# The causal mask as the first instead of the last product of each score bank in two key-block attentions

## The chip, the cores and the metric

The kernel runs on one core of a Trainium2 chip. The metric is the device time of one execution in microseconds, smaller is better. The kernel before took 2220.15 us as the median of three runs (2218.11 to 2220.37).

## What is computed

A float32 transformer of a first block (forgetting attention and stick-breaking attention side by side, then a mixture of 16 experts) and two more layers, the second of which mixes tokens with a native sparse attention (NSA). 512 tokens, width 1024. The change touches two attentions. The forgetting attention has 8 heads of 64:

```
logits = einsum(q, k) * scale + F[t] - F[s]      # F: running sum of log forget gates
logits = where(kpos <= qpos, logits, -inf)
out    = softmax(logits) @ v
```

NSA has 16 heads in 4 groups and adds three attentions by gates: over compressed keys, over selected key blocks and over a window. With 512 tokens there are 8 blocks of 64 and 16 may be selected, and the window is 512 wide, so the last two are plain causal attentions over their own keys and values, with a slope on the distance:

```
sc = einsum(q_blk, ks) * scale - slopes * dist
sc = where(dist >= 0, sc, NEG)
p  = softmax(sc)
```

## The kernel before

All engines run one long program each; the order of the work on each is the order in which it is written out, and semaphores join them. TensorE (PE) makes all products. To keep float32 accuracy a product is split in high and low parts (fp32r, one cycle a column), for instance the helper at L1729 with its three products; a product of two plain float32 tiles runs in two passes of two cycles a column.

Both attentions work by key blocks of 128 keys. For head h and key block j, a score bank (a PSUM bank, 128 keys by the 512 - 128 j queries from the block on) collects three products: the high keys with the high queries (L1990 in the forgetting attention, L2487 in NSA), the low terms (L1991, L2488), and a mask (L1995, L2495), which is an identity `IDB` as weights times `LKB`, 128x128 in bfloat16, with large negative numbers where a key lies after a query. It touches only the first 128 columns, the block on the diagonal. Its semaphore (`fs_done`, `s_done`) lets ScalarE (ACT) take the exponential (L1082, L1484) into `PROB`. The weighted product (L2004, L2514) of plain float32 `PROB` with the values follows two blocks later in the forgetting attention and three blocks later in NSA. Three score banks are used in turn; the scores of block n wait for the exponential of block n - 3.

The row of maxima that goes into the queries of a head is made two heads ahead: maxima products (L1947, L2438; for the compressed keys L2431) into another bank, CMB masks (L1956, L2449: `IDB` times `CMB`, bfloat16) on top, a reduction on VectorE (DVE, L2880, L3474), four small products that turn the maxima into a row (L1968, L2461), and a copy by ACT (L1062, L1439). L1980 and L2470 spread weights over partitions. ACT also moves finished outputs (L1070, L1071, L1449, L1450).

One turn n of the loop before: score products of block n, maxima products for head h + 2 (forgetting: turns 0 to 2 of 4; NSA: turns 0 to 6 of 9, turn 6 without CMB masks), the LKB mask of block n, the CMB masks, sometimes a spread or the row of maxima, then the weighted product of the older block. In NSA blocks 0 to 3 and 4 to 7 of a head are the two causal branches, block 8 the compressed one, which has no LKB mask. The last two heads have no maxima left to make.

The choice of banks relies on the first product of a bank with `start=True`: it opens the whole bank, and a later product writes what has not been written since and adds elsewhere. The maxima banks already use that.

Of the kernel before, what the change touches and what calls it, by code (L numbers as in the profile page):

```python
# [29 lines left out]
P = 128  # L30
D = 1024
T = 512
# [132 lines left out]
def program(nc, a, out):  # L165


    def sb(name, shape, dt=F32):
        return nc.alloc_sbuf_tensor(name, shape, dt)

    def sem(name):
        return nc.alloc_semaphore(name)
# [20 lines left out]
    IDB = sb("IDB", [P, P], BF16)  # L193
# [20 lines left out]
    PB = [nc.alloc_psum_tensor(f"PB{i}", [P, T], F32) for i in range(8)]  # L214
# [67 lines left out]
    def slot(n, kk=KK, width=W):  # L282
        if kk == KK and width == W:
# [22 lines left out]
    fs_done, fp_done, fpv_blk, fo_free = (sem(f"fox_{x}") for x in  # L306
                                                   ("scores", "probs", "block_used", "out_moved"))
# [36 lines left out]
    s_done, p_done, pv_blk, o_free = (sem(f"nsa_{x}") for x in ("scores", "probs", "block_used", "out_moved"))  # L344
# [89 lines left out]
    LKB = sb("LKB", [P, P], BF16)  # L434
# [13 lines left out]
    def over(name, start, shape, dt=F32):  # L448

        return nc.alloc_sbuf_tensor_at(name, shape, dt, offset=start)  # L450
# [33 lines left out]
    NQA, NQB = over("NQA", ht_at, [P, 4, T], F32R), over("NQB", htl_at, [P, 4, T], F32R)  # L484
# [15 lines left out]
    FKA, FKB = over("FKA", big_at, [P, NH1, T], F32R), over("FKB", big_at + 4096 * F, [P, NH1, T], F32R)  # L500
    FQA, FQB = over("FQA", big_at + 8192 * F, [P, 4, T], F32R), over("FQB", big_at + 10240 * F, [P, 4, T], F32R)
# [19 lines left out]
    NSA_BLOCKS = [(h, b, j) for h in range(NSA_H) for b in range(3) for j in range(1 if b == 2 else NT)]  # L521
# [12 lines left out]
    with block as blk:  # L534
# [1145 lines left out]
        def _(pe):  # L1680
# [136 lines left out]
            for d in range(ND):  # L1817
                if d > 5:
                    pe.wait_ge(n_ht[0], d - 5)
                for i in range(NT):  # L1820
                    if d == 0:
                        pe.wait_ge(n_xn, i + 1)
                    ins = pe.transpose(PB[XT_BANK[d]][:, i * P:(i + 1) * P], XN[:, i, d * P:(d + 1) * P], IDENT[:, :])
# [97 lines left out]
            for k in range(ND):  # L1921
                for n, (w, x) in enumerate(((FWH, HTH), (FWH, HTL), (FWL, HTH))):
                    ins = pe.matmul(PB[4][0:NH1, :], w[:, k, :], x[:, k, :], start=(k == 0 and n == 0),
                                    stop=(k == ND - 1 and n == 2))
# [14 lines left out]
            def fox_maxima(h, turn):  # L1939

                n = 3 * h + turn
                bank = PB[1 + n % 2]
                if n >= 2:
                    pe.wait_ge(fm_max, n - 1)
                for i in MAX_PARTS[turn]:
                    at_ = 384 if (turn, i) == (1, 0) else 0
                    pe.matmul(bank[:, at_:at_ + (i + 1) * P], FQA[:, h % 4, i * P:(i + 1) * P],  # L1947
                              FKA[:, h, 0:(i + 1) * P], start=(i == MAX_PARTS[turn][0]), stop=False, skip_group_check=True)

            def fox_max_masks(h, turn):  # L1950

                n = 3 * h + turn
                bank = PB[1 + n % 2]
                for i in MAX_PARTS[turn]:
                    at_ = 384 if (turn, i) == (1, 0) else 0
                    ins = pe.matmul(bank[:, at_ + i * P:at_ + (i + 1) * P], IDB[:, :], CMB[:, :], start=False, stop=True,  # L1956
                                    skip_group_check=True)
                ins.then_inc(fm_done, 1)
# [23 lines left out]
            def fox_scores(n):  # L1982

                h, j = FOX_BLOCKS[n]
                dst, q0 = PB[(0, 3, 4)[n % 3]][:, 0:T - j * P], j * P
                if n >= 3:
                    pe.wait_ge(fp_done, n - 2)
                if j == 0:
                    pe.wait_ge(fm_row, h + 1)
                pe.matmul(dst, FKA[:, h, q0:q0 + P], FQA[:, h % 4, q0:T], start=True, stop=False)  # L1990
                pe.matmul(dst, FKB[:, h, q0:q0 + P], FQB[:, h % 4, q0:T], start=False, stop=False)  # L1991

            def fox_score_mask(n):

                pe.matmul(PB[(0, 3, 4)[n % 3]][:, 0:P], IDB[:, :], LKB[:, :], start=False, stop=True).then_inc(fs_done, 1)  # L1995

            def fox_weighted(n):

# [21 lines left out]
            for n in range(len(FOX_BLOCKS) + 2):  # L2020
                h, t = n // NT, n % NT
                if n < len(FOX_BLOCKS):
                    fox_scores(n)
                    if h + 2 < NH1 and t < 3:
                        if t == 0:
                            pe.wait_ge(fq_ready, h + 3)
                        fox_maxima(h + 2, t)
                    fox_score_mask(n)
                    if h + 2 < NH1 and t < 3:
                        fox_max_masks(h + 2, t)  # L2030
                    if 1 <= h < NH1 - 1 and t == 1:
                        fox_max_T(h + 1)
                    if (h, t) in SPREAD_AT:
                        fox_spread(SPREAD_AT[h, t])
                if n >= 2:
                    fox_weighted(n - 2)
# [80 lines left out]
            for half in range(2):  # L2117
                g, q0 = GR["gates"] + 4 * half, 12 * half
# [57 lines left out]
            ins = pe.matmul(PB[5][:, 0:NT * EXPERTS], ONES[:, 0:P], chosen, start=True, stop=True)  # L2176
# [114 lines left out]
            for k in range(ND):  # L2291
                for n, (w, x) in enumerate(((KRH, HTH), (KRH, HTL), (KRL, HTH))):
                    ins = pe.matmul(PB[4][0:32, :], w[:, k, :], x[:, k, :], start=(k == 0 and n == 0),
                                    stop=(k == ND - 1 and n == 2))
# [49 lines left out]
            for m in range(2):  # L2344
                pe.wait_ge(m_qn if m == 0 else m_kn, 1 if m == 0 else 1 + NT)
                for h in range(MLA_H):
# [5 lines left out]
                    for i in range(NT):  # L2352
                        src = QN[:, i, h * QK_D:(h + 1) * QK_D] if m == 0 else KN[:, i, h, :]
                        ins = pe.transpose(PB[h][0:QK_D, i * P:(i + 1) * P], src, IDENT[:, :])
# [30 lines left out]
            for k in range(ND):  # L2385
                for n, (w, x) in enumerate(((SWGH, HTH), (SWGH, HTL), (SWGL, HTH))):
                    ins = pe.matmul(PB[0][0:48, :], w[:, k, :], x[:, k, :], start=(k == 0 and n == 0),
                                    stop=(k == ND - 1 and n == 2))
# [31 lines left out]
            for m in range(2):  # L2420
                ins = pe.transpose(PB[2][0:DH, m * CMP_LEN:(m + 1) * CMP_LEN], PER[:, m, :], IDENT[0:CMP_LEN, 0:CMP_LEN])
# [50 lines left out]
            def scores(n):  # L2472

                h, b, j = NSA_BLOCKS[n]
                if n >= 3:
                    pe.wait_ge(p_done, n - 2)
                if b == 0 and j == 0:
                    pe.wait_ge(mrow_ready, h + 1)
                grp = h // NSA_R
                if b == 2:  # L2480
                    dst, q0 = PB[n % 3][0:96, :], 0
                    keys = (t[:, grp, :, :].rearrange("p r n -> p (r n)") for t in (KCA, KCB))
                else:
                    dst, q0 = PB[n % 3][:, 0:T - j * P], j * P
                    keys = NKA[:, b * NSA_G + grp, q0:q0 + P], NKB[:, b * NSA_G + grp, q0:q0 + P]
                high, low = keys
                pe.matmul(dst, high, NQA[:, h % 4, q0:T], start=True, stop=False)  # L2487
                ins = pe.matmul(dst, low, NQB[:, h % 4, q0:T], start=False, stop=(b == 2))  # L2488
                if b == 2:
                    ins.then_inc(s_done, 1)  # L2490

            def score_mask(n):

                if NSA_BLOCKS[n][1] < 2:
                    pe.matmul(PB[n % 3][:, 0:P], IDB[:, :], LKB[:, :], start=False, stop=True).then_inc(s_done, 1)  # L2495

            def weighted(n):

# [18 lines left out]
            def token_products(m, l):  # L2517

                z = ZS[m][:, :, 2 * l:2 * l + CMP_STRIDE * (NCMP - 1) + 1:CMP_STRIDE]
                dst = PB[m][0:DH, 0:NSA_G * NCMP].rearrange("p (a b) -> p a b", a=NSA_G)  # L2520
                return pe.matmul(dst, CWS[:, m, l, :], z, start=(l == 0), stop=(l == CMP_LEN // 2 - 1))  # L2521
# [14 lines left out]
            for l in range(CMP_LEN // 2):  # L2536
                ins = token_products(0, l)
# [5 lines left out]
            for l in range(CMP_LEN // 2):  # L2543
                ins = token_products(1, l)
# [5 lines left out]
            for m in range(2):  # L2550
                for l in range(CMP_LEN // 2):
                    ins = position_products(m, l)
# [3 lines left out]
            for turn_no in range(len(SECOND_MAXIMA_AT), 6):  # L2556
# [3 lines left out]
                      start=True, stop=True).then_inc(c_mm, 1)  # L2560
            for q in range(NSA_G):
                ins = pe.matmul(PB[6][0:NCMP, q * DH:(q + 1) * DH], HD[:, 1, q, :], CW2[:, 1, :], start=True, stop=True)
# [7 lines left out]
            for n in range(len(NSA_BLOCKS) + 3):  # L2570
                h, t = n // PER_HEAD, n % PER_HEAD
                if n < len(NSA_BLOCKS):
                    scores(n)
                    if h + 2 < NSA_H and t < len(MAX_TURNS):
                        if t == 0:
                            pe.wait_ge(q_ready, h + 3)
                        maxima(h + 2, *MAX_TURNS[t])
                    score_mask(n)
                    if h + 2 < NSA_H and t < len(MAX_TURNS):
                        max_masks(h + 2, *MAX_TURNS[t])  # L2580
                    if h % 2 and h >= 3 and t in (1, 3, 5):
                        spread((h - 3) // 2, t // 2)
                    if h + 2 < NSA_H and t == PER_HEAD - 1:
                        max_T(h + 2)
                if n >= 3:
                    weighted(n - 3)
# [1006 lines left out]
```

## Time and profile before

| | |
|---|---|
| median of three runs | 2220.15 us |
| span of the profiled execution | 2216.6 us (3.55 us below the median; the runs' times take in what lies around the span) |
| PE busy | 96% of the span |
| ACT, DVE busy | 43%, 55% |
| forgetting attention, key blocks | about 121 to 162 us |
| NSA, key blocks | about 1623 to 1801 us |

Times in the rows count from the span's start. Each matmul appears twice: its weight load on PEld and its product on PE. The product's recorded duration runs to the end of its results, so that following products overlap; the distance from one start to the next is the better measure of what a product takes.

### The profile page before, as it was taken

The numbers are of one execution on the slowest core, as the hardware profiler recorded it, in microseconds if no ns is written. First come the engines' busy times: TensorE is split into PE (matmuls) and PEld (weight loads), VectorE is DVE, ScalarE is ACT, GpSimd is POOL, SyncE is SP. The second block draws the span as 40 slices with busy tenths as digits, with TensorE's granted clock in tenths as the row PEclk, the third lists the DMA queues.
The fourth block names the chain that finished last, engine by engine and source line by source line (L and its number), as shares of the span: only waits on it lengthen the run. The fifth ranks groups of instructions, "written<-read, shape, count | busy, mean of one in ns | idle before, by whom it ended". The sixth has DMA issues, their size and how long they took to land.

```text
span 2216.6 us, 25820 instructions
## 1 busy us (share of the span) xinstructions
PE 2132.4 (96%) x10108; PEld 1670.4 (75%) x10108; DVE 1211.2 (55%) x1702; ACT 953.0 (43%) x1484; POOL 188.3 (8%) x239
## 2 busy tenths in 40 slices
PE   8999999999999968999999999999999999999998
PEld 4768678867676647887878888878877767888887
DVE  6747654477777745367544454453446555445444
ACT  4455532346655524236431134343357765112343
POOL 2240001101000010000000000020223200000000
PEclk9999999999999988999999999999989999999999
DMA  9405035939999973220223322232100012332221
GB/s 350 162 25 177 9 127 176 364 133 354 383 379 373 383 270 99 91 79 27 77 90 104 101 95 95 95 106 95 60 1 3 3 50 86 98 102 94 102 99 58
DMA packets 153080, 309.05 MB, mean 139 GB/s; under 512 B 15062, under 2 KB 16619, under 8 KB 152957
## 3 DMA queue, kind: packets, MB, share of 16 engines
q1 hardware_dynamic: 122788, 229.98, 30.4%
q0 software_dynamic: 11648, 41.60, 4.9%
q10 hardware_dynamic: 18524, 35.81, 4.6%
q8 instruction: 81, 1.33, 0.2%
q14 instruction: 39, 0.32, 0.0%
HBM read 275.97 MB, written 30.99 MB: 138 GB/s over the span
## 4 chain that ended last, share of the span: by engine, by line
PE 84%; DVE 7%; DMA 4%; ACT 4%; issue 1%; POOL 0%; SPq 0%; ACTq 0%; DVEq 0%; POOLq 0%
PE PB L1729 60%; PE PB L2246 4%; PE PB L2514 3%; DMA BIG<-in_expert_w_down 3%; PE PB L2488 1%; PE PB L2438 1%; PE PB L2487 1%; PE PB L1881 1%; PE PB L1902 1%; PE PB L2004 1%; DVE WL L2657 1%; PE PB L2186 1%; PE PB L2521 1%; PE PB L2075 1%; DMA X<-in_x 1%
## 5 line engine op out<-in xcount | busy, mean ns | idle before, releaser
L2657 DVE TENSOR_TENSOR WL<-RING,WH 128x1024 fp32r<-128x1024 f32 x228 | 280.7, 1231 | 595.2 <-ACT WH L970 384.3
L970 ACT CAST WH<-RING 128x1024 fp32r<-128x1024 f32 x228 | 239.4, 1050 | 769.2 <-PE PB L1729 764.4
L1729 PE MATMUL PB<-HTH,WH 128*128 128x512 f32 x1056 | 412.2, 390 | 4.8 <-DVE HTL L2684 3.7
L1729 PE MATMUL PB<-HTL,WH 128*128 128x512 f32 x1056 | 411.0, 389 | 0.0
L1729 PE MATMUL PB<-HTH,WL 128*128 128x512 f32 x1056 | 410.9, 389 | 0.0
L1729 PEld LDWEIGHTS PB<-HTH,WH 128*128 128x128 f32 x1056 | 198.4, 188 | 48.1 <-issue 5.5
L1729 PEld LDWEIGHTS PB<-HTH,WL 128*128 128x128 f32 x1056 | 198.3, 188 | 41.5
L1729 PEld LDWEIGHTS PB<-HTL,WH 128*128 128x128 f32 x1056 | 198.4, 188 | 40.3
L1729 PE MATMUL PB<-WH,NHH 128*128 128x512 f32 x496 | 193.2, 390 | 1.8 <-DVE NHL L2662 1.8
L1729 PE MATMUL PB<-WL,NHH 128*128 128x512 f32 x496 | 193.0, 389 | 0.0
L1729 PE MATMUL PB<-WH,NHL 128*128 128x512 f32 x496 | 193.0, 389 | 0.0
L3051 DVE TENSOR_TENSOR EWL<-RING,EWH 128x1024 fp32r<-128x1024 f32 x128 | 151.8, 1218 | 50.3 <-ACT EWH L1186 49.9
L1186 ACT CAST EWH<-RING 128x1024 fp32r<-128x1024 f32 x128 | 130.7, 1049 | 86.6 <-PE PB L1729 71.6
L1729 PE MATMUL PB<-EWH,HTL 128*128 128x512 f32 x512 | 166.9, 407 | 0.0
L1729 PEld LDWEIGHTS PB<-EWH,HTL 128*128 128x128 f32 x512 | 93.9, 188 | 24.1 <-issue 6.7
L1729 PEld LDWEIGHTS PB<-WH,NHH 128*128 128x128 f32 x496 | 93.1, 188 | 21.7 <-DVE NHL L2662 2.6
L2246 PE MATMUL PB<-BIG,NAT 128*128 128x512 f32 x240 | 106.7, 594 | 2.4 <-DMA BIG<-in_expert_w_down 2.3
L1729 PEld LDWEIGHTS PB<-WH,NHL 128*128 128x128 f32 x496 | 93.1, 188 | 19.4
L1729 PEld LDWEIGHTS PB<-WL,NHH 128*128 128x128 f32 x496 | 93.1, 188 | 19.4
L1729 PE MATMUL PB<-WH,HTL 128*128 128x512 f32 (+1 forms) x296 | 99.6, 367 | 1.0 <-DVE BIG L3376 1.0
L1729 PE MATMUL PB<-EWL,HTL 128*128 128x512 f32 x256 | 100.3, 392 | 0.0
L2514 PE MATMUL PB<-PROB,NVA 128*128 128x512 f32 (+3 forms) x256 | 95.7, 456 | 1.7 <-ACT RST L1450 1.0
(594 smaller groups left out, 3453.5 us busy)
## 6 DMA issues: line engine op xcount, KB each, us to landing
RING<-in_mlp_w SPq DMA_DIRECT2D x64, 1024.0 KB, 5.1
RING<-in_expert_w_gate SPq DMA_DIRECT2D x32, 1024.0 KB, 7.8
RING<-in_expert_w_up SPq DMA_DIRECT2D x32, 1024.0 KB, 12.0
BIG<-in_expert_w_down ACTq DMA_DIRECT2D x30, 1024.0 KB
RING<-in_w_in SPq DMA_DIRECT2D x20, 1024.0 KB, 5.2
BIG<-in_ada_w SPq DMA_DIRECT2D x9, 2048.0 KB, 13.8
dispatch_rows<-BIG POOLq DMA_DIRECT2D x24, 512.0 KB, 18.6
RING<-in_a_w_in SPq DMA_DIRECT2D x10, 1024.0 KB, 5.1
```

Of the source, the lines that this page charges most:

```text
L970: ins = nc.scalar.copy(split_weights(stage, q)[0], halves_of(n, q))
L1186: nc.scalar.copy(EWH[:, q % MOE_SLOTS], halves_of(CH["moe"] + GU_AT[e] + j // 2, j)).then_inc(high_ready, 1)
L1729: yield pe.matmul(dst, lhs, rhs, start=(start and n == 0), stop=(stop_ and n == 2))
L1881: ins = pe.matmul(PB[u % 4][:, 0:nk + nk % 2], lhs, rhs, start=(n == 0), stop=(n == len(pairs) - 1))
L1902: ins = pe.matmul(PB[6 + u % 2][:, 0:DH], PT[0:n, u % 2, j, :], v(it, h, b, j, n), start=(j == 0), stop=(j == len(m) - 1))
L2004: ins = pe.matmul(PB[5 + h % 2][:, j * P:T], v, PROB[:, n % 4, 0:T - j * P], start=(j == 0), stop=(j == NT - 1))
L2075: ins = pe.matmul(PB[3 + 4 * (p % 2)][half, i * P:(i + 1) * P], SV[:, j, h * DH:(h + 1) * DH], SPT[:, u % 4, j, :], start=(j == 0), stop=( ...
L2186: ins = pe.matmul(PB[banks[d // 4]][:, (d % 4) * P:(d % 4 + 1) * P], NAT[:, i, d * P:(d + 1) * P], hits[:, i, :], start=(i == 0), stop=(i ...
L2246: ins = pe.matmul(PB[5 + m][:, :], ACTT[e % 2][:, k, :], w[:, k, :], start=(k == 0), stop=(k == KK - 1))
L2514: ins = pe.matmul(dst, lhs, rhs, start=(j == 0), stop=last)
L2657: return V.tensor_tensor(wl, halves_of(n, q), wh.bitcast(F32), ALU.subtract)
L3051: V.tensor_tensor(EWL[:, q % MOE_SLOTS], halves_of(CH["moe"] + GU_AT[e] + j // 2, j), EWH[:, q % MOE_SLOTS].bitcast(F32), ALU.subtract).th ...
```

## The change

The LKB mask product moves from behind the maxima products to the first place of its turn. It opens the bank (`start=True`), both score products add to it, and the low product closes it and gives the semaphore. The block with compressed keys is as before. `skip_group_check=True` concerns the build alone.

```diff
@@ forgetting attention, fox_scores
-                pe.matmul(dst, FKA[:, h, q0:q0 + P], FQA[:, h % 4, q0:T], start=True, stop=False)
-                pe.matmul(dst, FKB[:, h, q0:q0 + P], FQB[:, h % 4, q0:T], start=False, stop=False)
-
-            def fox_score_mask(n):
-
-                pe.matmul(PB[(0, 3, 4)[n % 3]][:, 0:P], IDB[:, :], LKB[:, :], start=False, stop=True).then_inc(fs_done, 1)
+                pe.matmul(dst[:, 0:P], IDB[:, :], LKB[:, :], start=True, stop=False, skip_group_check=True)
+                pe.matmul(dst, FKA[:, h, q0:q0 + P], FQA[:, h % 4, q0:T], start=False, stop=False, skip_group_check=True)
+                pe.matmul(dst, FKB[:, h, q0:q0 + P], FQB[:, h % 4, q0:T], start=False, stop=True,
+                          skip_group_check=True).then_inc(fs_done, 1)
@@ its loop, between the maxima products and the CMB masks
-                    fox_score_mask(n)
@@ NSA, scores
-                pe.matmul(dst, high, NQA[:, h % 4, q0:T], start=True, stop=False)
-                ins = pe.matmul(dst, low, NQB[:, h % 4, q0:T], start=False, stop=(b == 2))
-                if b == 2:
-                    ins.then_inc(s_done, 1)
-
-            def score_mask(n):
-
-                if NSA_BLOCKS[n][1] < 2:
-                    pe.matmul(PB[n % 3][:, 0:P], IDB[:, :], LKB[:, :], start=False, stop=True).then_inc(s_done, 1)
+                if b < 2:
+                    pe.matmul(dst[:, 0:P], IDB[:, :], LKB[:, :], start=True, stop=False, skip_group_check=True)
+                pe.matmul(dst, high, NQA[:, h % 4, q0:T], start=(b == 2), stop=False, skip_group_check=True)
+                pe.matmul(dst, low, NQB[:, h % 4, q0:T], start=False, stop=True, skip_group_check=True).then_inc(s_done, 1)
@@ its loop, between the maxima products and the CMB masks
-                    score_mask(n)
```

## Rows read from the trace of the kernel before

**Rows 1.** The page: span, busy time, and the chain that ended last by engine.

```profile
span 2216.6 us, 25820 instructions
PE 2132.4 (96%) x10108; PEld 1670.4 (75%) x10108; DVE 1211.2 (55%) x1702; ACT 953.0 (43%) x1484; POOL 188.3 (8%) x239
PE 84%; DVE 7%; DMA 4%; ACT 4%; issue 1%; POOL 0%; SPq 0%; ACTq 0%; DVEq 0%; POOLq 0%
```

**Rows 2.** Busy time by stretch (us), with counts, granted PE clock, DMA share, GB/s.

```profile
121.00:162.00 41.00, 39.66 (x240) 28.18 (x241) 16.76 (x29) 25.64 (x54) 13.91 (x18) 1.00 0.01 2
1623.00:1801.00 178.00, 176.19 (x1042) 131.18 (x1042) 96.23 (x206) 133.67 (x267) 41.28 (x48) 0.98 0.02 3
```

**Rows 3.** Waits, 1623 to 1801: who waited for whom: us, times, longest.

```profile
ACT PROB L1484 <- PE PB L2495: 38.0, 62, 1.5
PEld PB L2487 <- ACT PROB L1484: 2.5, 10, 0.3
PE PB L2514 <- ACT RST L1450: 1.0, 2, 0.7
PE PB L2461 <- ACT NQA L1439: 0.8, 1, 0.8
```

**Rows 4.** Timeline, weight loads, 1685.9 to 1687.3: start, us, what.

```profile
1686.17 0.10 PEld L2495 LDWEIGHTS PB<-LKB,IDB 128*128 128x128 bf16 x1
1686.19 0.15 PEld L2449 LDWEIGHTS PB<-CMB,IDB 128*128 128x128 bf16 x2
1686.30 0.30 PEld L2514 LDWEIGHTS PB<-PROB,NVA 128*128 128x128 f32 x2
1686.73 0.19 PEld L2487 LDWEIGHTS PB<-NQA,NKA 128*128 128x128 f32 x1
1687.06 0.19 PEld L2488 LDWEIGHTS PB<-NQB,NKB 128*128 128x128 f32 x1
```

**Rows 5.** Timeline, 1689.25 to 1689.66: a mask with no CMB masks behind it.

```profile
1689.34 0.19 PEld L2488 LDWEIGHTS PB<-NQB,NKB 128*128 128x128 f32 x1
...
1689.52 0.10 PEld L2495 LDWEIGHTS PB<-LKB,IDB 128*128 128x128 bf16 x1
...
1689.52 0.31 PEld L2514 LDWEIGHTS PB<-PROB,NVA 128*128 128x128 f32 x2
```

**Rows 6.** Chain that ended last, 1786 to 1801 (NSA heads 14 and 15).

```profile
1795.49 0.46 ACT OUP L1449
...
1796.57 1.04 ACT CWH L1457
```

**Rows 7.** Turn 3 of even heads: timeline about 1695.5, chain at first and last.

```profile
1695.16 0.57 ACT L1450 COPY RST<-PB 1x512 f32<-1x512 f32 x1
...
1695.48 0.10 PEld L2449 LDWEIGHTS PB<-CMB,IDB 128*128 128x128 bf16 x1
...
1695.85 0.30 PEld L2514 LDWEIGHTS PB<-PROB,NVA 128*128 128x128 f32 x2 [0.27 <-issue]
...
1650.50 0.12 issue
...
1763.61 0.12 issue
```

**Rows 8.** Chain, 120 to 162: L1990 at turn 0 of heads 1 to 5.

```profile
125.51 0.23 PE PB L1990
...
130.44 0.47 PE PB L1990
...
135.60 0.35 PE PB L1990
...
140.66 0.47 PE PB L1990
...
145.82 0.35 PE PB L1990
```

**Rows 9.** Busy time by stretch as in rows 2; granted clock third from the end.

```profile
1620.00:1640.00 20.00, 19.02 (x105) 14.44 (x105) 8.70 (x20) 11.49 (x22) 3.43 (x4) 0.79 0.00 1
1640.00:1660.00 20.00, 19.88 (x122) 14.87 (x121) 8.62 (x21) 14.70 (x31) 6.11 (x8) 1.00 0.02 3
```

## The prediction

> **What bounds the kernel now.** I read first the page, to see which engine sets the time: TensorE (PE) is busy in 96% of a span of 2216.6 us and makes up 84% of the chain that ended last [rows 1]. Then the stretches in which the changed lines run: 121 to 162 us (forgetting attention, 8 heads of 4 key blocks) and 1623 to 1801 us (the 16 NSA heads, 9 blocks each). PE is busy for 39.7 of 41 and 176.2 of 178 us, ScalarE (ACT) for 25.6 and 133.7 [rows 2]. In both stages one turn of the loop is: score products, maxima products two heads ahead, masks, weighted product of an older block. The waits of the NSA stage name ACT waiting for the score mask (38.0 us, 62 times), but PE's weight loads waiting for an exponential only for 2.5 us and PE for a moved output or row 1.8 us [rows 3]. So the exponential has slack, and what counts is how many nanoseconds of PE each turn takes. An earlier score bank is worth little; an order that costs PE more is paid in full.
>
> **How PE's turn is read.** Busy matmul rows overlap and say nothing of spacing; the weight loads (PEld) do. The load of the next matmul begins when the matmul before begins to stream. In [rows 4] L2487 is loaded at 1686.73, while the second pass of L2514 streams 384 columns at two cycles each (0.32 us); L2488 is loaded at 1687.06: no gap, the f32 load is hidden. Where a 128-column matmul is in front, it is not: after the last CMB load (the second of the pair from 1686.19, so about 1686.24) the first L2514 load follows at 1686.30, one mask's streaming later (0.06), but its second load only 0.11 after that (two loads of 0.19 take 0.30 in all). A load of f32 weights thus takes 0.11 us of PE where no longer matmul covers it; a bf16 load takes no more than the 0.06 us that a mask streams.
>
> **A mask in company and a mask alone.** In company (LKB mask, then CMB masks) another bf16 mask costs 0.06 us: it shifts the rest by its own columns, and the one uncovered f32 load is paid by the last mask whoever that is. Alone between two f32 matmuls, as at the turns without CMB masks [rows 5]: L2488 is loaded at 1689.34, so streams from 1689.45 (0.11 later, its own load being uncovered) to 1689.50 (128 columns, 0.05). The mask's load starts only then, at 1689.52; the next f32 matmul's second load, the start of its streaming, is at 1689.64 (0.31 less 0.19 after 1689.52). So from stream to stream a lone mask costs 0.13 us.
>
> **The change part by part.** The products are the same: 160 masks, 160 pairs of score products, no DMA, nothing else on another engine. Opening the bank with 128 columns and adding the products to it I cost at nothing, since the second product already adds to a bank at its column count. The waits (probability, row of maxima) stay ahead of the turn's first matmul, now the mask: nothing new queues behind them. What moves is the mask.
> 1. Turns with CMB masks: 6 of 9 in NSA heads 0 to 13 (84), 3 of 4 in forgetting heads 0 to 5 (18). The mask leaves its company (-0.06) and stands alone between L2514 (L2004) and L2487 (L1990), whose load was hidden (+0.13): +0.075 each by the unrounded spacing. 84 give 6.3 us, 18 give 1.35.
> 2. Turns whose mask was alone already, behind a 128-column product: NSA turns 6 and 7 of heads 0 to 13 (28), forgetting turn 3 of heads 0 to 5 (6). Before: 0.05 + 0.13 from the last product's start to the next. After: 0.11, for the f32 load behind 128 columns is still uncovered. Minus 0.07, plus 0.13 in front: +0.06 each, 1.7 and 0.35 us. Turns of NSA heads 14 and 15 with 256 or more columns change place with place: nothing; there the chain runs through ACT (0.46 OUP, 1.04 CWH) anyway [rows 6], so their 128-column turns cost nothing either.
> 3. Stalls that this fills. At turn 3 of every second NSA head (2 to 12, six times) L2514 waits for ACT to move the output of the branch before: the CMB load is at 1695.48, L2514's at 1695.85 instead of 1695.54, 0.12 after the RST copy ends; the chain shows the same 0.12 of issue at 1650.50 and 1763.61, first and last of the six [rows 7]. Two turns lie between that branch's last product and the wait; PE comes 0.15 us later and waits 0.15 less: -0.9 us. In the forgetting stage L1990 stands on the chain for 0.47 us (130.44, 140.66) or 0.35 (135.60, 145.82) where it needs 0.23 (125.51) [rows 8]: it waits for its row of maxima. A mask that comes first takes over that gap; ACT's row comes no later and PE arrives later: -0.7 us.
> 4. The first 8 us of the NSA stage run at half clock (granted 0.79 over 1620 to 1640, 1.00 after) [rows 9]: the exposed loads double there for half a head, +0.2 us.
>
> Sum: 6.3 + 1.7 - 0.9 + 1.35 + 0.35 - 0.7 + 0.2 = **+8.3 us**. After both stages the chain goes on with PE's split matmuls, so it arrives whole: the profiled span would be 2224.9, and the median, 3.5 us above this span, 2220.15 + 8.3 = 2228.4 us.
>
> **The bounds.** No row shows a bf16 load behind a plain-f32 matmul of two passes (L2514), nor a lone mask ahead of L2487. From below, the mask costs 0.06 there as in company: items 1 and 2 vanish or turn slightly negative, about 2219 to 2220 us. From above, the whole recorded f32 load (0.19) lies open behind the mask: 0.20, that is 0.07 more in 136 turns, +9.5, about 2238 us. I take 0.13: rows 5 are the same pair, mask before f32, and the bf16 load that begins only at the end of a stream is seen after f32 products whatever their width.
> The Trainium skill, "TensorE: Matmul & The Clock Gate" (Step-by-step: what each phase is for), says that PE pulls the next weight load ahead of matmuls in flight into a background buffer, so that it runs under the current one. Taken alone this would hide the mask's load and leave only its streaming, the lower bound; rows 4 show it for f32 behind long matmuls, rows 5 show it failing for a bf16 load behind f32.
>
> **Rivals.**
> - **No change (chance 0.12).** The switch is free in the new place: L2514's passes are long (128 to 512 columns, two cycles each) and may cover the bf16 load and, with it, part of the next. A lone mask then costs 0.06, the sum is 0 to +2: 2219 to 2222. For it: rows 4, hidden f32 load. Against it: rows 5, and a 128-column mask cannot cover a load of 0.11.
> - **Faster (0.05).** The score banks close before the maxima instead of after them: on average 427 columns (0.18 us) and a mask earlier, in 102 turns. If PE were waiting for probabilities in most turns, up to 0.23 x 102 = 23 us would come back; less 9.9 of added load, 13.6 us faster, 2206.6. It decides once PE waits for exponentials in about half of the turns (0.23 x 51 is more than 9.9). The rows give 2.5 us in all for that wait [rows 3], so only PE idle that the profile does not show could bring it.
> - **Slower through the clock (0.07).** The stage begins with some 8 us at half clock [rows 9]; a PE with more gaps could stay there as long again, which costs half of it, +4.2: 2232.6.
> - **Forecast (0.76)**, its own range 2224 to 2232.
>
> **How the numbers follow.** A measurement of this kernel tells about 0.2% (4.4 us) from nothing. Slower by more than that, over 2224.6, takes nearly all of the forecast and the clock case: 0.82. Within: the no-change case and the forecast's low edge, 0.13. Faster: 0.05. The range leaves out the far ends of the bounds and the faster case: 2222 to 2234.
>
> **What would show it.** In the NSA stage after: the mask's load (now ahead of the products) begins as L2514's second pass ends, and the load of the low product comes about 0.13 us later, where before the high product's load lay hidden. A head without half clock or spread differences takes some 0.5 us more; PE busy rises by little, the stage by 7 us, the forgetting stage by 1. ACT's wait for the scores falls. At turn 3 the 0.12 of issue shrinks or goes. I am wrong if the low product's load follows the mask's by 0.06, if the stage does not lengthen, or if it lengthens with the spacings unchanged (then a wait or the clock did it).

## The result and the profile after

The change is slower: 2224.15 us (median of ten runs, 2219.94 to 2229.33) against 2219.3 us for the kernel before (ten runs, 2218.11 to 2222.29): 4.85 us between the medians, a ratio of 1.0021 with a 95% interval of 1.0011 to 1.0030, that is +4.7 us. The forecast was 2228.4 us in a range of 2222 to 2234: right sign, inside the range, but +8.3 us where 4.7 to 4.85 came.

The page of the changed kernel, as [rows 1]; the profiled execution took 2219.94 us, the lowest of the ten:

```profile
span 2218.3 us, 25820 instructions
PE 2134.0 (96%) x10108; PEld 1665.1 (75%) x10108; DVE 1211.8 (55%) x1702; ACT 953.4 (43%) x1484; POOL 187.5 (8%) x239
PE 84%; DVE 7%; ACT 4%; DMA 4%; issue 1%; POOL 0%; SPq 0%; ACTq 0%; DVEq 0%; POOLq 0%
```

Its span is only 1.7 us above that of before, because it won 2.5 us in stretches that the change does not touch: 1.4 us ahead of the forgetting stage and 1.1 us between the two stages. The table of stretches, with the granted clock third from the end, of the changed kernel and then of the kernel before:

```profile
0.00:120.00 120.00, 105.66 (x464) 72.78 (x465) 80.60 (x122) 55.25 (x87) 34.18 (x43) 0.99 0.71 245
1620.00:1640.00 20.00, 19.29 (x104) 14.05 (x105) 7.62 (x16) 13.36 (x25) 3.43 (x4) 0.85 0.01 1
```

```profile
0.00:120.00 120.00, 108.07 (x456) 74.97 (x456) 79.19 (x120) 55.05 (x86) 32.68 (x43) 0.96 0.71 245
```

The granted clock of the first 120 us was 0.99 against 0.96, and the NSA stage began 2.1 us sooner (first low product's load at 1621.3 against 1623.4). So whole spans can't carry the comparison; the stages can. From the load of the first low product to that of the last, the NSA stage takes 181.0 us (177.2 before) and the forgetting stage 39.15 (38.77): +3.8 and +0.4, together 4.2, near the difference of the medians. To keep the half clock of the stage's start out, I use NSA heads 2 to 13 below, from low product to low product. First the changed kernel, then the one before (length of the stretch, then PE busy):

```profile
1645.02:1784.25 139.23, 139.23 (x825) 99.50 (x823) 80.58 (x174) 101.93 (x205) 37.11 (x43) 1.00 0.02 3
```

```profile
1646.63:1782.36 135.73, 135.00 (x824) 101.71 (x823) 80.59 (x174) 101.30 (x205) 37.24 (x43) 1.00 0.02 3
```

The same products take 3.5 us more in twelve heads, and the 0.73 us in which PE had nothing to do are gone (six times the 0.12 of [rows 7]).

**The lone mask.** Weight loads of the changed kernel at the beginning of a head, as [rows 4]:

```profile
1644.15 0.30 PEld L2506 LDWEIGHTS PB<-PROB,NVA 128*128 128x128 f32 x2
1644.59 0.10 PEld L2485 LDWEIGHTS PB<-LKB,IDB 128*128 128x128 bf16 x1
1644.91 0.19 PEld L2486 LDWEIGHTS PB<-NQA,NKA 128*128 128x128 f32 x1 [0.22 <-issue]
1645.02 0.19 PEld L2487 LDWEIGHTS PB<-NQB,NKB 128*128 128x128 f32 x1
```

The mask (L2485) is loaded at 1644.59, where L2506's second pass begins, and its load runs under that pass: 0.32 us (384 columns at two cycles) before the high product's load at 1644.91, which marks the mask's first column. The low product's load follows 0.11 later, at the high product's first column. So a lone mask behind a two-pass f32 product costs 0.11 us: the f32 load behind it lies open, its own load does not. I had taken 0.13, from a mask behind an fp32r product [rows 5].

**The stall at turn 3.** At turn 3 of every second head the weighted product waits until ACT has moved out the finished output of the branch before. PE's loads and ACT's work over turns 1 to 3 of head 6, changed kernel, in order of time (turn 1's low product at 1692.80 and weighted product at 1693.45, turn 3's at 1694.74 and 1695.27):

```profile
1692.80 0.19 PEld L2487 LDWEIGHTS PB<-NQB,NKB 128*128 128x128 f32 x1
...
1693.35 0.49 ACT L1484 ACTIVATE PROB<-PB 128x384 f32<-128x384 f32 x1 [0.35 <-PE PB L2487]
...
1693.45 0.30 PEld L2506 LDWEIGHTS PB<-PROB,NVA 128*128 128x128 f32 x2
...
1693.99 0.58 ACT L1449 COPY OUP<-PB 64x512 f32<-64x512 f32 x1
...
1694.58 0.57 ACT L1450 COPY RST<-PB 1x512 f32<-1x512 f32 x1
...
1694.74 0.19 PEld L2487 LDWEIGHTS PB<-NQB,NKB 128*128 128x128 f32 x1
...
1695.27 0.30 PEld L2506 LDWEIGHTS PB<-PROB,NVA 128*128 128x128 f32 x2
```

And before:

```profile
1693.21 0.19 PEld L2488 LDWEIGHTS PB<-NQB,NKB 128*128 128x128 f32 x1
...
1693.91 0.30 PEld L2514 LDWEIGHTS PB<-PROB,NVA 128*128 128x128 f32 x2
...
1694.06 0.49 ACT L1484 ACTIVATE PROB<-PB 128x384 f32<-128x384 f32 x1 [0.48 <-PE PB L2495]
...
1694.57 0.58 ACT L1449 COPY OUP<-PB 64x512 f32<-64x512 f32 x1
...
1695.02 0.19 PEld L2488 LDWEIGHTS PB<-NQB,NKB 128*128 128x128 f32 x1
```

Before, the exponential of turn 1 began 0.85 us after the turn's low product began, when the maxima and the mask were through, and the output's copy stood right behind it in ACT's order (0.49 later, 1694.55 to 1694.57). After, the exponential begins after 0.55 us, and the copy no longer waits for it. From turn 1's weighted product to turn 3's it was 1.94 us before (1693.91 to 1695.85 [rows 7]) and is 1.82 now. The chain's 0.12 of issue at this place is gone: turn 3 runs into turn 4 without it.

```profile
1695.37 0.07 PE PB L2446
1695.44 0.96 PE PB L2506 x2
```

From low product to low product, turn 3 of even heads takes 1.60 us against 1.80.

**The forgetting stage.** The chain at turn 0 of heads 1, 2 and 3, as [rows 8] (L1990 is now the mask, L1991 the high product):

```profile
124.16 0.28 PE PB L1991
...
129.23 0.14 PE PB L1990
129.37 0.28 PE PB L1991
...
134.45 0.06 PE PB L1990
134.51 0.28 PE PB L1991
```

The high product takes 0.28 everywhere, 0.05 more than the 0.23 of before, since its load lies open behind the mask. At head 2 the mask stands for 0.14 instead of 0.06: 0.08 us of waiting are left of the 0.24 of before (0.47 less 0.23). At head 3 nothing is left of 0.12. By the loads, heads 4 and 6 are like head 2 and head 5 is like head 3, so the five gaps gave back 0.7 us.

### The profile page after: what moved, and what is told of

It reads as the page before. It is cut to its first block, busy times and chain, and to the rows that moved or that the text cites. A ratio compares the mean times of both kernels' runs of the same rounds, so it can differ in the third digit from the quotient of the medians.

```text
span 2218.3 us, 25820 instructions
## 1 busy us (share of the span) xinstructions
PE 2134.0 (96%) x10108; PEld 1665.1 (75%) x10108; DVE 1211.8 (55%) x1702; ACT 953.4 (43%) x1484; POOL 187.5 (8%) x239
## 4 chain that ended last, share of the span: by engine, by line
PE 84%; DVE 7%; ACT 4%; DMA 4%; issue 1%; POOL 0%; SPq 0%; ACTq 0%; DVEq 0%; POOLq 0%
PE PB L1729 60%; PE PB L2243 4%; PE PB L2506 3%; DMA BIG<-in_expert_w_down 3%; PE PB L2486 1%; PE PB L2487 1%; PE PB L2435 1%; PE PB L1881 1%; PE PB L1902 1%; DVE WL L2648 1%; PE PB L2002 1%; PE PB L2183 1%; PE PB L2072 1%; PE PB L2513 1%; DMA X<-in_x 1%
## 5 line engine op out<-in xcount | busy, mean ns | idle before, releaser
L2506 PE MATMUL PB<-PROB,NVA 128*128 128x512 f32 (+3 forms) x256 | 95.1, 454 | 1.0 <-ACT RST L1450 0.9
```

The source lines that it names most:

```text
L2506: ins = pe.matmul(dst, lhs, rhs, start=(j == 0), stop=last)
```

## The experiments

Two things were to be told apart: what a mask costs by its neighbours, and whether the stall at turn 3 shrinks because PE comes later or because the bank closes earlier. All times of turns below are from the load of one low product to that of the next, so that the time of a turn holds the opening mask of the next one; in heads that do the same work they repeat within about 0.01 us. "NSA, heads 2 to 13" is 135.7 us before and 139.2 in the change. The ratios are to runs of the kernel before that were taken with the experiment. Those of the first two experiments and of the change overlap in their intervals; what tells them apart are the turns and stages of one trace each.

**Mask closing the bank, ahead of the maxima.**

```diff
                     scores(n)
+                    score_mask(n)
                     if h + 2 < NSA_H and t < len(MAX_TURNS):
...
                         maxima(h + 2, *MAX_TURNS[t])
-                    score_mask(n)
```

The same in the forgetting attention.

> The kernel before, but the mask, still the last product of its bank, stands between the score products and the maxima products. The bank closes as early as in the change, and the mask is alone between two fp32r products. Price theory: a lone bf16 mask costs 0.13 us from stream to stream behind fp32r (its load starts only when that stream has ended), against 0.11 behind the two-pass f32 product as in the change. So turns 0 to 5 of NSA take 0.075 us more than before (0.02 at turn 3) against the change's 0.057, heads 0 to 13 together +6.4 us before stalls. Bank theory (the early closed bank brings ACT's chain forward, so that the wait at turn 3 of even heads shrinks by some 0.25 us): low product to low product at turn 3 about 1.6 us as in the change, NSA stage (first low product's load to the last, 177.2 us before, 181.0 in the change) 182.0. Lateness theory (PE merely comes later to the wait): turn 3 falls by 0.15 less its own 0.02, stage 182.5. Rival: if the mask's load were free behind fp32r too, the turns take 0.05 more and the stage is 180.5.

Measured: ratio 1.0028 (1.0018 to 1.0038). NSA stage 182.25 us, heads 2 to 13 139.6. Turns with CMB masks took 0.07 to 0.08 more than before (0.01 at turn 3 of odd heads, which has no stall), against 0.05 to 0.07 in the change. The stage lies halfway between the two theories' 182.0 and 182.5 and does not decide between them. The loads of a turn:

```profile
1696.43 0.19 PEld L2488 LDWEIGHTS PB<-NQB,NKB 128*128 128x128 f32 x1
1696.78 0.10 PEld L2495 LDWEIGHTS PB<-LKB,IDB 128*128 128x128 bf16 x1 [0.16 <-issue]
1696.79 0.31 PEld L2438 LDWEIGHTS PB<-NKA,NQA 128*128 128x128 f32 x2
```

Behind the fp32r product the mask's load does wait for the stream's end: 1696.78, with the next f32 load 0.01 behind. The second of the pair, L2438's first column, is at 1696.91 (0.31 less 0.19 later): 0.13 as in [rows 5]. So both prices are real and it is the neighbour in front that decides. Turn 3 of even heads took 1.60 us, as in the change: more than lateness alone was to give (1.67), so the early bank has a part in it.

**Maxima between the opening mask and the scores.**

```diff
                 if b < 2:
                     pe.matmul(dst[:, 0:P], IDB[:, :], LKB[:, :], start=True, ...)
+                maxima_between()
                 pe.matmul(dst, high, NQA[:, h % 4, q0:T], start=(b == 2), ...)
```

> The change, but the maxima products stand between the opening mask and the score products: the mask is alone in the same place and costs the same 0.11 us, while the bank closes as late as in the kernel before. Bank theory: the order's price is unchanged (+0.057 a turn), but the wait at turn 3 of even heads shrinks only by PE's lateness, 0.11: turn 3 from low product to low product stays 1.70 to 1.80 us (1.80 before, 1.60 in the change), NSA stage 181.9, and in the forgetting stage the turn 0 gap shrinks as in the change or a little less. Lateness theory: as the change, turn 3 1.60 us, stage 181.0.

Measured: ratio 1.0031 (1.0017 to 1.0044). Turn 3 of even heads stayed at 1.77 us, and the copy of the output again stood right behind the exponential:

```profile
1700.47 0.49 ACT L1484 ACTIVATE PROB<-PB 128x384 f32<-128x384 f32 x1 [0.64 <-PE PB L2492]
1700.99 0.58 ACT L1449 COPY OUP<-PB 64x512 f32<-64x512 f32 x1
```

From turn 1's weighted product to turn 3's it is 1.92 us (1700.35 to 1702.27), near the 1.94 of before and not the 1.82 of the change. So the late bank is enough to bring most of the stall back, although PE comes as late as in the change. (The maxima of a turn now fall into the time of the turn before; odd heads, without the stall, take 1.78 us for turn 3 here and in the change, so that 1.77 against 1.60 is the stall.)

The stage took 182.7 us, 0.8 more than I expected and 1.7 over the change, of which the stall is about 1.0 (6 x 0.17). The rest shows in the loads. At turn 1 the last maxima product has 128 columns, and the high product stands behind it:

```profile
1699.64 0.19 PEld L2439 LDWEIGHTS PB<-NKA,NQA 128*128 128x128 f32 x1
1699.82 0.19 PEld L2491 LDWEIGHTS PB<-NQA,NKA 128*128 128x128 f32 x1
1699.92 0.19 PEld L2492 LDWEIGHTS PB<-NQB,NKB 128*128 128x128 f32 x1
```

The high product's load takes 0.11 us there, where 128 columns cover only 0.055. Turn 4 has the same; turn 3 has one such open load fewer, since 512 columns of maxima now stand between the mask and the high product. That is some 0.05 us a head, 0.7 in 14 heads, by my estimate from these rows.

**Two opening masks.**

```diff
                     pe.matmul(dst[:, 0:P], IDB[:, :], LKB[:, :], start=True, ...)
+                    pe.matmul(dst[:, 0:P], IDB[:, :], LKB[:, :], start=False, ...)
```

This adds the mask twice, which leaves the sense of the output as it is and adds a product to 160 turns.

> The change with the opening mask product issued twice (the score banks get the mask twice). Prices a mask in company at the same place: 0.056 us each by its columns. Price theory: every turn with a mask in heads 0 to 13 takes 0.056 more, 112 turns, +6.3 us less up to 0.05 x 12 of stall, NSA stage 186.7 to 187.3; forgetting stage +1.2. Rival (a mask is priced by a load of its own, 0.11): +12 us, stage 193. Rival (the f32 load behind it hides it): stage 181, no change.

Measured: ratio 1.0047 (1.0031 to 1.0064; four runs), NSA stage 187.4 us (+6.4 over the change), forgetting stage 40.3 (+1.2). The loads at a turn's beginning:

```profile
1701.28 0.10 PEld L2487 LDWEIGHTS PB<-LKB,IDB 128*128 128x128 bf16 x1
1701.34 0.19 PEld L2488 LDWEIGHTS PB<-NQA,NKA 128*128 128x128 f32 x1
1701.44 0.19 PEld L2489 LDWEIGHTS PB<-NQB,NKB 128*128 128x128 f32 x1
```

The second mask shifts the rest by its own columns, 0.055 to 0.06 (1701.28 to 1701.34), and the f32 load behind it still lies open for 0.11. That is the price in company, at the very place where the first one costs 0.11. This run also shows PE's lateness at work: turn 3 of odd heads took 0.05 more than in the change (1.83 against 1.78), turn 3 of even heads 1.60 as in the change. The second mask filled the last 0.05 us of the stall there.

**Opening the next bank in the CMB masks' company.** At turns with CMB masks the bank of the next block is opened right behind them; block 0 and block 7, and the last two heads, keep the place of before.

```diff
-                if NSA_BLOCKS[n][1] < 2:
+                if NSA_BLOCKS[n][1] < 2 and not opened_ahead(n):
...
                     score_mask(n)
                     if h + 2 < NSA_H and t < len(MAX_TURNS):
                         max_masks(h + 2, *MAX_TURNS[t])
+                    if opened_ahead(n + 1):
+                        open_bank(n + 1)
```

> Where a turn has CMB masks and the next block has a mask, the next bank is opened right behind the CMB masks, in their company (NSA blocks 1 to 6, forgetting blocks 1 to 3 of the heads with maxima); the others keep the place they have in the kernel before. Banks close early, no mask is alone except NSA block 7 and those of the last two heads. Price theory: turns 0 to 5 as before, turn 6 0.075 less (a lone mask saved), so -1.05 us over 14 heads, plus the bank theory's 0.25 or more at turn 3 of six heads: NSA stage 174.7 us against 177.2 before and 181.0 in the change; forgetting stage 1 us less than before; together some 3.5 us faster than the kernel before, ratio 0.998. Rival: the opening mask waits for the exponential of two blocks earlier, one weighted product sooner than before; if ACT is that late in several turns of a head, the stage is as long as before or longer.

Measured: 2219.65 us against 2219.96, ratio 0.9998 (0.9989 to 1.0007): no difference that can be told. NSA stage 176.8 us, heads 2 to 13 135.3, half a microsecond under before. I had miscounted: turn 0 now holds two masks, +0.055, against turn 6 without one, -0.074, so a head gains 0.02 and not 0.075. Turn 3 of even heads fell to 1.675 us, 0.13 less, not 0.25. The forgetting stage gained nothing (38.99): its turn 3 saved nothing from head 1 on, since the gap at the next turn 0 took it back. The rival's stall (the earlier wait for the exponential) did not show in heads 2 to 11. Head 12 lost 0.32 us at turn 8, where PE waited for a reduction on VectorE, and head 13 0.11 at turn 1; I did not follow why.

**Six openers.** The kernel before, with the mask as opener only at turn 1 of heads 2, 4, 6, 8, 10 and 12.

```diff
+            def opens(n):
+
+                h, t = n // PER_HEAD, n % PER_HEAD
+                return t == 1 and h % 2 == 0 and 2 <= h <= 12
...
+                if opens(n):
+                    pe.matmul(dst[:, 0:P], IDB[:, :], LKB[:, :], start=True, stop=False, skip_group_check=True)
```

> The kernel before, with the mask as opener only at turn 1 of the NSA heads 2, 4, 6, 8, 10 and 12: six masks instead of 160. At this turn the weighted product whose output ACT must move by turn 3 is issued last, so a longer turn 1 makes PE no later between it and the wait. Bank theory (the exponential of block 1 starts earlier because its bank closes before the 512 columns of maxima, and the move comes behind it in ACT's order): turn 3 of these heads falls from 1.80 to about 1.60 us or lower (1.49 is what it takes without a wait), turns 1 cost 0.057 each: NSA stage from 177.2 to 176.3 us, perhaps 175.8. Lateness theory (only PE coming later fills the wait): turn 3 stays 1.80, the six turns cost 0.057 each, stage 177.6. Either way less than a measurement of the whole kernel can tell: ratio 0.999 to 1.000.

Measured: 2218.41 us against 2220.53, ratio 0.9993 (0.9984 to 1.0002). Turn 3 of these heads took 1.67 us, 0.13 less, with PE no later than before. The stage took 176.4 us, but 0.55 of the 0.87 lies in head 0, which the edit does not touch; heads 2 to 13 gained 0.34:

```profile
1647.11:1782.50 135.39, 135.39 (x824) 101.39 (x822) 80.63 (x174) 101.57 (x205) 37.34 (x43) 1.00 0.02 3
```

ACT's rows, and the weighted products of turns 1 and 3:

```profile
1694.22 0.49 ACT L1484 ACTIVATE PROB<-PB 128x384 f32<-128x384 f32 x1 [0.28 <-PE PB L2495]
...
1694.33 0.30 PEld L2521 LDWEIGHTS PB<-PROB,NVA 128*128 128x128 f32 x2
...
1694.86 0.58 ACT L1449 COPY OUP<-PB 64x512 f32<-64x512 f32 x1
...
1696.14 0.30 PEld L2521 LDWEIGHTS PB<-PROB,NVA 128*128 128x128 f32 x2
```

The exponential is early (0.55 after the low product's load at 1693.67), and the copy now starts 0.15 after it ends, no longer at once: what holds it is the branch's last weighted product (the profile names it for the same copy in the kernel with the mask in the middle). From that product to turn 3's it is 1.81 us, as good as the 1.82 of the change. An earlier bank alone therefore gives 0.13 and no more. In the change another 0.12 comes from PE's later arrival: in the same stretch its own work is 0.12 to 0.13 us longer, opening masks of 0.11 and 0.13 (turn 3's stands behind an fp32r weighted product) for two masks of 0.055. Together that is the 0.26 which the change takes from this stall of 0.31 (turn 3 is 0.20 shorter though it holds 0.055 more). So the two theories were not rivals; each has half.

## Why the prediction came out as it did

- **What bounds the stages, right.** PE's order set the time: in heads 2 to 13 of the changed kernel PE is busy for all 139.23 us. The earlier banks shortened ACT's waits for scores (31.5 to 27.5 us between 1640 and 1785), which gave PE nothing back except at turn 3.
- **The direction and the mechanism, right.** A mask leaves its company, where it costs 0.055 (two openers), and stands alone, where the f32 load behind it lies open. The no-change rival's premise, a mask that costs 0.06 alone, fell with the loads of the changed kernel.
- **The size of item 1, the step that failed.** I wrote "I take 0.13: rows 5 are the same pair", and that the bf16 load beginning only at a stream's end "is seen after f32 products whatever their width". That holds after fp32r products (mask in the middle: 0.13), and no bf16 load stood behind a two-pass product in either attention before. After a two-pass f32 product, which stands in front of 7 of 8 openers in a head, the load is hidden and the price is 0.11. I had also said that the mask's load would begin as the second pass ends; it begins as that pass begins. Turns took 0.05 to 0.06 more where that product is in front, and 0.06 to 0.075 where the opening mask of turn 3 stands behind the one fp32r weighted product. For 84 + 18 turns the term comes to about 5.9 us instead of 7.65.
- **Item 2, the same error.** The change costs about 0.036 at each of these turns, not 0.06: 28 + 6 turns, 1.2 us instead of 2.05. It is a -0.075 for the mask that leaves and a +0.11 for the one in front.
- **Item 3, too small, for half a reason.** The stall at turn 3 gave back 0.26 six times, 1.5 us, not 0.9. I had it shrink by PE's lateness alone (0.15; it gave 0.12 to 0.13). I left out that the copy stood behind an exponential which the change brings forward, and had written that an earlier bank is worth little. The forgetting stage's gaps gave back what I said, 0.7.
- **Item 4** (half clock) can't be judged: the stretch at half clock was shorter in this execution (granted 0.85 over 1620 to 1640 against 0.79 [rows 9]).
- **The sum** with these sizes: 5.9 + 1.2 - 1.5 - 0.7, 4.9 us, against 4.2 in the two stages and 4.7 to 4.85 in the medians. The stages' own ends hold the difference to 4.2: NSA heads 0 and 1 grew by 0.19 and 0.30 us where the items ask for 0.42 each, and heads 14 and 15, which I had at nothing, got 0.22 us shorter together. The forecast also started from 2220.15 us, the median of the first three runs; ten runs gave 2219.3, and that 0.85 us is in the miss of 4.25 on the time.
- The Trainium skill, "TensorE: Matmul & The Clock Gate" (Step-by-step: what each phase is for), has PE pull the next weight load under the current matmul. The runs show that for f32 loads behind long products (1687.06 [rows 4]) and for a bf16 load behind a two-pass f32 product (1644.59); they show the contrary for a bf16 load behind an fp32r product (1696.78). The rule, which I had set aside wholly for this load, was right for the place the mask moved to.

## What to carry to other kernels

Price a small bf16 product by its neighbours, not by its columns: here it cost 0.055 us beside its like, 0.11 alone behind a two-pass f32 product and 0.13 alone behind an fp32r product, so 160 of them reordered made 4 to 5 us. Half of the 0.11 is the mask's own columns, the other half is the part of the f32 load behind it that they do not cover. Handing a result over earlier paid here only where the engine that takes it was late for something that PE waited for: six openers at the one such turn took 0.13 us each from the stall and cost 0.055 each, and neither that kernel nor the one that opens banks in company could be told from the kernel before as a whole. Compare stages from like instruction to like instruction: the profiled span alone would have said +1.7 us.

## What was not expected of the hardware

The load of bf16 weights starts under a running product of plain f32, one whole pass ahead: in the changed kernel the opening masks' loads stand 0.11, 0.21, 0.32 and 0.43 us ahead of their first columns behind products of 128, 256, 384 and 512 columns, but for a few turns with a wait in front. In none of these traces does it start under an fp32r product: for all 128 NSA masks of the kernel before, behind 128 to 512 columns, and for the 15 openers of turn 3 after, it begins within 0.01 us of its own first column. Why the two differ, no run here shows.
